# Moving the splits, gate rests and gate steps at the expert stages' seams, and the dilated values into the queries' and keys' block

## The chip, the cores and the metric

The kernel runs on one core of one Trainium2 chip. The metric is the device time of one launch in microseconds (us); lower is better.

## The reference

Two transformer layers on x of 512 tokens by 1024, in float32. The second layer begins with attention of two kinds over one projection, and both layers end with the same kind of expert stage (PEER), which the change touches most. Cut to what matters:

```python
def peer_ffn(h, w_query, sub_keys, expert_u, expert_v):
    def chunk(xc):                                   # 128 tokens
        q = (xc @ w_query).reshape(128, 8, 2, 128)
        s1 = einsum('thc,hnc->thn', q[:, :, 0], sub_keys[:, 0])
        s2 = einsum('thc,hnc->thn', q[:, :, 1], sub_keys[:, 1])
        v1, i1 = lax.top_k(s1, 16)
        v2, i2 = lax.top_k(s2, 16)
        cand = (v1[..., :, None] + v2[..., None, :]).reshape(128, 8, 256)
        top, ci = lax.top_k(cand, 16)
        eidx = e1 * 128 + e2                         # e1, e2: the chosen i1, i2
        gate = jax.nn.softmax(top, axis=-1)
        act = gelu(einsum('td,thkd->thk', xc, expert_u[eidx]))
        return einsum('thk,thkd->td', gate * act, expert_v[eidx])

# second layer, first half
h = rms_norm(x, norm1_g) * (1 + sc1) + sh1
qa, ka, va, qb, kb, vb, gl = jnp.split(h @ w_in, IN_SPLITS, axis=-1)
qa, ka = rope(rms_norm(qa)), rope(rms_norm(ka))      # dilated window attention, values va
qb, kb = rope(rms_norm(qb)), rope(rms_norm(kb))      # differential attention, values vb
```

There are 16384 experts, of which each of 8 heads picks 16 per token.

## The kernel before, in words

The program is one sequence of blocks; in a block, each engine has its own queue, in program order, and waits on semaphores; between two blocks all engines meet at a barrier (L83). Matmuls of float32 values are made of three with rounded halves: a tile is split into a high half (a cast on ScalarE) and a low half (a subtraction on VectorE), and hi*hi, lo*hi and hi*lo are added up.

**The expert stage** (`peer`, names p1 and p2 for the two layers) handles the first token tile (128 tokens) by fetching its experts' rows, and the other 384 tokens (DENSE) densely: all 128 tiles of 128 experts are multiplied with all 384 tokens, and a gate array that is zero for experts not chosen picks among them. Its blocks:

- `peer_queries` (p1q, p2q): the queries, then a `TurnedBack` guest.
- `peer_choose` (p1c, p2c): for each of four token tiles, TensorE makes 16 score products, and VectorE finds the top 16 by MAX8, FIND_INDEX8 and MATCH_REPLACE8. Between these steps stand the low-half splits of expert tiles, `A.split_lo` (L1429), at 14 places per token tile (EARLY); TensorE multiplies 14 tiles per token tile (`A.multiply`, L1439, output pre, double buffered), ScalarE takes them by a gelu (L1421), casts the high half of the tile four further on (L1410), and issues the store of the result (L1398). At the end of the choosing of a token tile, TensorE turns the choice (`turn`), and ScalarE copies it to the rows first, second and gate (L1557).
- `peer_gates` (p1g, p2g): the other 72 tiles, in 12 pieces (PIECES) of 6 tiles (LATE) and 8 steps (STEPS). A step makes one-hot rows of four tokens on VectorE (L1760, L1762), their rests on ScalarE (L1797), 8 products on TensorE (L1787) and a copy of the result by ScalarE (L1815). `steps_after(i)` says which steps follow tile i of a piece. Before the first step, `rest_of_gates` computes for all 384 tokens what rounding took from the gates (L1739 to L1745). VectorE also takes fetched expert rows (`fetch.take`, L1334, L1342), which GpSimd gathers (L1319). SyncE loads tile n + 4 when tile n has been split (L1389), and stores finished pieces.
- `peer_values` (p1v, p2v): for each of the 128 tiles, VectorE makes the weights w (L1908, L1910), w and the value tile are split (L1894, L1896, L1913, L1916), and TensorE adds up (L1931), after a rehearsal of ten small matmuls (L127).

In `peer_gates` the split order is one tile ahead at most: the first instruction of VectorE in the block is the split of the block's first tile.

**The second layer's start** (`block2`): `queries_keys` (qk) multiplies in 9 chunks of 512 columns (seven of queries and keys, two of the differential values vb), each of 8 slabs; the queries and keys are normed, rotated on VectorE (scratch prod, rot; tables rope) and turned. Four PSUM banks take the output, ScalarE copies each to raw (L3021). Then a `product` block of its own (va) makes the dilated values in two chunks, of 256 and of 512 columns (the latter with strided token tiles), eight banks, copies by ScalarE and VectorE (L361, L362), its SyncE also loading the masks. Then comes the dilated attention (dat).

What sets the order around the change is program order in these functions, by hand.

Of the kernel before, what the change touches and what calls it, by code (L numbers as in the profile page):

```python
# [1246 lines left out]
def peer(nc, tag, C, hT, ring, handed, wq, keysT, u_tab, u_rows, v_tab, gates, acts, take):  # L1247
# [3 lines left out]
    with ExitStack() as whole:  # L1251
# [4 lines left out]
        A = Activations(nc, whole, tag + "a", x_hi, x_lo, u_tab, acts)  # L1256
        with ExitStack() as mid:
# [5 lines left out]
            peer_choose(nc, tag + "c", C, qT, keys, rows, A, fetch)  # L1263
        kept = sbo("kept", [P, KEPT_PIECES, KEYS, PIECE])
        W = Weights(nc, whole, tag + "w", gates, acts, v_tab, A)
        peer_gates(nc, tag + "g", C, rows, gates, kept, A, W, fetch)
# [3 lines left out]
class Fetched:  # L1270
# [31 lines left out]
    def steps(self, tile):  # L1302

        late = KEYS - TT * EARLY
# [140 lines left out]
class Weights:  # L1445
# [4 lines left out]
    LOADS, G = 4, EGROUP  # L1450
    STORED = DENSE // PIECE - KEPT_PIECES

    def __init__(self, nc, ctx, tag, gates, acts, v_tab, A):
        sb, _, sem = phase_tools(nc, ctx, tag)
        self.gates, self.acts, self.v_tab, self.A = gates, acts, v_tab, A
        self.v = A.u
# [5 lines left out]
        self.w_made, self.v_ready = sem("w_made"), sem("v_ready")  # L1462
# [17 lines left out]


EARLY = 14


def peer_choose(nc, tag, C, qT, keys, rows, A, fetch):
# [4 lines left out]
    with ExitStack() as ctx:  # L1490
# [13 lines left out]
        chosen = sb("chosen", [P, 2, PAIRS])  # L1504
# [4 lines left out]
        gate = sb("gate", [P, PHEADS, TOPK])  # L1509
# [10 lines left out]
        @block.sync  # L1520
        def _(sp):
            for n in range(A.LOADS, TT * EARLY + A.LOADS):
                A.load(sp, n)

        def turn(pe, t):
            pe.wait_ge(chosen_ready, t + 1)
            if t >= 2:
                pe.wait_ge(moved, 3 * (t - 1))
            for n, src in enumerate((chosen[:, 0, :], chosen[:, 1, :], gate[:].rearrange("p h k -> p (h k)"))):
                last = nc.tensor.transpose(tp[:, n, 0:P], src, C["ident"][:])  # L1530
            last.then_inc(turned, 1)

        @block.tensor
        def _(pe):
# [15 lines left out]
            turn(pe, TT - 1)  # L1550

        @block.scalar
        def _(act):
# [15 lines left out]
            take_rows(TT - 1)  # L1569

        @block.vector
        def _(dve):
            n = 0
            for t in range(TT):
                dve.wait_ge(scored, t + 1)
# [3 lines left out]
                A.split_lo(dve, t * EARLY)  # L1579
                dve.wait_ge(step, n)  # L1580
                for j in range(HALVES):
                    if j == HALVES // 2:
                        A.split_lo(dve, t * EARLY + 1)
# [6 lines left out]
                A.split_lo(dve, t * EARLY + 2)  # L1590
# [4 lines left out]
                A.split_lo(dve, t * EARLY + 3)  # L1595
# [3 lines left out]
                A.split_lo(dve, t * EARLY + 4)  # L1599
# [13 lines left out]
                A.split_lo(dve, t * EARLY + 5)  # L1613
                dve.wait_ge(step, n)
                for h in range(PHEADS):
                    if h == PHEADS // 2:
                        A.split_lo(dve, t * EARLY + 6)
# [4 lines left out]
                A.split_lo(dve, t * EARLY + 7)  # L1622
# [10 lines left out]
                A.split_lo(dve, t * EARLY + 8)  # L1633
# [34 lines left out]
                for s in range(2):  # L1668
# [4 lines left out]
                    A.split_lo(dve, t * EARLY + 9 + 2 * s)  # L1673
# [5 lines left out]
                    A.split_lo(dve, t * EARLY + 10 + 2 * s)  # L1679
# [6 lines left out]
                A.split_lo(dve, t * EARLY + 13)  # L1686
# [15 lines left out]
def peer_gates(nc, tag, C, rows, gates, kept, A, W, fetch):  # L1702
# [10 lines left out]
    LATE = (KEYS - TT * EARLY) // PIECES  # L1713
    STORED = PIECES - KEPT_PIECES
    base = TT * EARLY
    with ExitStack() as ctx:
# [3 lines left out]
        gate_hi = hot1[:, 0].rearrange("p q k -> p (q k)")[:, 0:DENSE]  # L1720
        spare = W.g[:, 1].rearrange("p a g t -> p (a g t)")
        gate_rest, floor, gate_top = (spare[:, n * DENSE:(n + 1) * DENSE] for n in range(3))
        prod = ps("prod", [P, RING, TOK, KEYS])
        A.place(ps)
        hot_ready, hot_free, prod_free = sem("hot_ready"), sem("hot_free"), sem("prod_free")
        step, top_made, rest_known, rest_ready = (sem(n) for n in ("step", "top_made", "rest_known", "rest_ready"))
        stored = [sem(f"stored{s}") for s in range(KEPT_PIECES)]
        block = ctx.enter_context(nc.Block())

        def steps_after(i):  # L1730

            return range(STEPS * i // LATE, STEPS * (i + 1) // LATE)

        def rest_of_gates(dve):

            V = nc.vector
            ch = Chain(dve, step)
            dve.wait_ge(top_made, 1)
            ch.add(V.tensor_copy(gate_top, gate_hi))  # L1739
            ch.add(V.tensor_scalar(floor, gate_hi, TINY, None, ALU.max))  # L1740
            ch.add(V.tensor_tensor(gate_rest, gate[:], gate_hi, ALU.subtract))
# [1612 lines left out]
```

## Time and profile before

| | |
|---|---|
| median of 3 runs | 3777.59 us (3773.73 to 3779.41) |
| the profiled execution, its own time | 3770.69 us |
| its span in the profile | 3768.9 us |
| TensorE busy | 3595.0 us, 95% |
| VectorE busy | 2971.7 us, 79% |
| ScalarE busy | 1723.8 us, 46% |
| GpSimd busy | 753.1 us, 20% |
| DMA | 853.50 MB, 226 GB/s on average |

The span is the time from the first to the last profiled instruction. Busy time of TensorE (PE) counts matmuls, whose ends are modelled: a row of 128x384 lasts longer than the distance to the next. The chain that ended last is in its final 14% the value matmuls of the second expert stage.

### The profile page before, as it was taken

To read this page: it belongs to the slowest core of one execution; us is meant where nothing else is said; L and a number is where in the kernel's file an instruction comes from. 1 tells how busy PE (TensorE), PEld (TensorE's weight loads), DVE (VectorE), ACT (ScalarE), POOL (GpSimd) and SP (SyncE) were. 2 spreads that over 40 slices of the span, in tenths; PEclk is the share of its full clock that TensorE was granted. 3 is DMA by queue.
4 is the path that set the end of the run, shared out by engine and by line. 5 is a ranking of instruction groups with operands and counts; after the bars stand their busy time and mean duration, and the time that the engine had idled before them with its cause. 6 is when DMAs were issued, how large, how long until landed. Compare 5 with 4: busy or idle time off the path is not lost. (4 is left out here: it accounts for less than half of the span.)

```text
span 3768.9 us, 54814 instructions
## 1 busy us (share of the span) xinstructions
PE 3595.0 (95%) x19530; PEld 3150.1 (84%) x19530; DVE 2971.7 (79%) x6556; ACT 1723.8 (46%) x3277; POOL 753.1 (20%) x523
## 2 busy tenths in 40 slices
PE   8868999999999999999899989899999999999999
PEld 7546788899999988888788757788999999888887
DVE  4674653998988799999676495546998888899998
ACT  4424443333666633333344564343335666433333
POOL 0000000000333344444100000000003333355542
PEclk9989999999999999999999999999999999999999
DMA  4352323445999899999522102323558999899997
GB/s 149 138 172 89 102 68 101 136 161 185 303 309 308 292 371 404 405 404 401 189 84 79 51 1 90 109 73 121 163 165 276 310 309 311 321 405 404 404 403 293
DMA packets 371888, 853.50 MB, mean 226 GB/s; under 512 B 35728, under 2 KB 184848, under 8 KB 368912
## 3 DMA queue, kind: packets, MB, share of 16 engines
q1 hardware_dynamic: 258912, 530.84, 40.2%
q0 software_dynamic: 73728, 268.47, 18.8%
q10 hardware_dynamic: 38976, 50.68, 4.0%
q8 instruction: 157, 2.57, 0.3%
q14 instruction: 115, 0.94, 0.1%
HBM read 753.26 MB, written 95.42 MB: 225 GB/s over the span
## 5 line engine op out<-in xcount | busy, mean ns | idle before, releaser
L1319 POOL DMA_INDIRECT p2f_row<-in_expert_u_rows,p2f_index x128 | 176.9, 1382 | 1299.5 <-POOLq L83 1027.9
L1319 POOL DMA_INDIRECT p1f_row<-in_peer_u_rows,p1f_index x128 | 172.9, 1351 | 966.8 <-POOLq L83 684.3
L1931 PE MATMUL p2v_out<-p2a_u_hi,p2v_w_hi 128*128 128x512 f32 x768 | 298.9, 389 | 0.4 <-DVE p2v_w_lo L1916 0.4
L1931 PE MATMUL p1v_out<-p1a_u_hi,p1v_w_hi 128*128 128x512 f32 x768 | 298.9, 389 | 0.4 <-DVE p1v_w_lo L1916 0.4
L1931 PE MATMUL p1v_out<-p1a_u_hi,p1v_w_lo 128*128 128x512 f32 x768 | 298.8, 389 | 0.0
L1931 PE MATMUL p2v_out<-p2a_u_hi,p2v_w_lo 128*128 128x512 f32 x768 | 298.8, 389 | 0.0
L1931 PE MATMUL p1v_out<-p1a_u_lo,p1v_w_hi 128*128 128x512 f32 x768 | 298.8, 389 | 0.0
L1931 PE MATMUL p2v_out<-p2a_u_lo,p2v_w_hi 128*128 128x512 f32 x768 | 298.8, 389 | 0.0
L1319 POOL DMA_INDIRECT p2f_row<-in_expert_v,p2f_index x128 | 201.1, 1571 | 238.0 <-DVE p2f_sum L1342 216.4
L1319 POOL DMA_INDIRECT p1f_row<-in_peer_v,p1f_index x128 | 197.0, 1539 | 237.5 <-DVE p1f_sum L1342 217.0
L1894 ACT CAST p2a_u_hi<-p2a_u 128x1024 fp32r<-128x1024 f32 x128 | 135.0, 1055 | 186.8 <-PE p2v_out L1931 169.4
L1894 ACT CAST p1a_u_hi<-p1a_u 128x1024 fp32r<-128x1024 f32 x128 | 135.0, 1055 | 177.9 <-PE p1v_out L1931 168.7
L1439 PE MATMUL p1g_pre<-p_x_hi,p1a_u_hi 128*128 128x384 f32 x576 | 198.0, 344 | 3.8 <-DVE p1a_u_lo L1429 3.8
L1439 PE MATMUL p2g_pre<-p_x_hi,p2a_u_hi 128*128 128x384 f32 x576 | 197.2, 342 | 3.8 <-DVE p2a_u_lo L1429 3.8
L1439 PE MATMUL p1g_pre<-p_x_hi,p1a_u_lo 128*128 128x384 f32 x576 | 194.2, 337 | 0.0
L1439 PE MATMUL p1g_pre<-p_x_lo,p1a_u_hi 128*128 128x384 f32 x576 | 194.1, 337 | 0.0
L1439 PE MATMUL p2g_pre<-p_x_hi,p2a_u_lo 128*128 128x384 f32 x576 | 193.7, 336 | 0.0
L1439 PE MATMUL p2g_pre<-p_x_lo,p2a_u_hi 128*128 128x384 f32 x576 | 193.2, 336 | 0.0
L1342 DVE SCALAR_TENSOR_TENSOR p2f_sum<-p2f_row,p2f_weight,p2f_sum 128x1024 f32<-128x1024 f32 x127 | 162.5, 1280 | 11.7 <-DMA p2f_row<-in_expert_v,p2f_index 10.5
L1342 DVE SCALAR_TENSOR_TENSOR p1f_sum<-p1f_row,p1f_weight,p1f_sum 128x1024 f32<-128x1024 f32 x127 | 162.6, 1280 | 11.5 <-DMA p1f_row<-in_peer_v,p1f_index 9.7
L1931 PEld LDWEIGHTS p1v_out<-p1a_u_hi,p1v_w_hi 128*128 128x128 f32 x768 | 144.2, 188 | 30.5 <-DVE p1a_u_lo L1913 0.6
L1931 PEld LDWEIGHTS p2v_out<-p2a_u_hi,p2v_w_hi 128*128 128x128 f32 x768 | 144.2, 188 | 30.4 <-DVE p2a_u_lo L1913 0.6
(760 smaller groups left out, 10785.5 us busy)
## 6 DMA issues: line engine op xcount, KB each, us to landing
p1a_u<-in_peer_u SPq DMA_DIRECT2D x128, 512.0 KB
p1a_u<-in_peer_v SPq DMA_DIRECT2D x128, 512.0 KB
p2a_u<-in_expert_u SPq DMA_DIRECT2D x128, 512.0 KB
p2a_u<-in_expert_v SPq DMA_DIRECT2D x128, 512.0 KB
gates<-p_kept SPq DMA_DIRECT2D x20, 2048.0 KB
acts<-p1a_a ACTq DMA_DIRECT2D x128, 192.0 KB
p1w_a<-acts SPq DMA_DIRECT2D x128, 192.0 KB
acts<-p2a_a ACTq DMA_DIRECT2D x128, 192.0 KB
```

Of the source, the lines that this page charges most:

```text
L1319: self.nc.gpsimd.indirect_dma_start(self.row[:, n % self.RING, :], None, self.u_rows if dot else self.v_rows, bass.IndirectOffsetOnAxis(ap ...
L1342: V.scalar_tensor_tensor(self.sum[:], row, weight, self.sum[:], ALU.mult, ALU.add).then_inc(self.used, 1)
L1439: last = self.nc.tensor.matmul(self.pre[:, n % 2, 0:DENSE], u[:, s, k * P:(k + 1) * P], x[:, k, P:SEQ], start=(m == 0), stop=(m == 3 * DK ...
L1894: nc.scalar.copy(v_hi[:, n % VSLABS, :], v[:, n % LOADS, :]).then_inc(v_hi_ready, 1)
L1931: last = nc.tensor.matmul(out[:, o, :], lhs[:, s, t * P:(t + 1) * P], rhs[:, n % VSLABS, cols], start=(n == 0 and m == 0), stop=(n == KEYS ...
```

## The change

Parts, in order of the program:

1. `choice`: the chosen numbers and the gates of a token tile (chosen, gate), before scratch of `peer_choose`, now lie in `fetch.sum`, so that they outlive the block.
2. `peer_choose`: VectorE splits tiles 0 and 1 ahead of the loop, and each later place splits the tile two further on (`first_split`). One tile more is multiplied in the block (tile 56; INTO = 57). The last turn and its row copies leave it.
3. `peer_gates`: 71 tiles. VectorE splits tile INTO + 1 + i at iteration i. TensorE turns the last choice behind its first tile; ScalarE copies the rows at i = 1; VectorE waits for them at i = 2. The gates are rounded and their rests made per 128 tokens, at i = 0, 16 and 40. The 96 steps follow tiles 1 to 70 evenly, none the first. Values 0 and 1 are split here, on ScalarE behind tile TILES - 2 and ahead of the last gelu, on VectorE at the end.
4. `peer_values`: the splits of values 0 and 1 are gone from its loop.
5. `queries_keys`: 11 chunks; the last two are the dilated values, copied to va by ScalarE. prod and rot lie in va, the rope tables in the masks' buffer, and the masks are loaded when all rotations are done. The va block is gone.

```diff
+EARLY, AHEAD = 14, 2
+INTO = TT * EARLY + 1
...
@@ peer_choose
-            turn(pe, TT - 1)
+            A.multiply(pe, TT * EARLY)
...
-            take_rows(TT - 1)
+            A.gelu(act, TT * EARLY)
...
+            for ahead in range(AHEAD):
+                A.split_lo(dve, ahead)
             for t in range(TT):
+                first_split = t * EARLY + AHEAD
                 dve.wait_ge(scored, t + 1)
                 for j in range(HALVES):
                     V.max(val[:, j // 2, j % 2, 0:8], score[:, j, :]).then_inc(step, 1)
                 n += HALVES
-                A.split_lo(dve, t * EARLY)
+                A.split_lo(dve, first_split)
...
@@ peer_gates
+            return range(ALL * max(i - 1, 0) // (TILES - 1), ALL * i // (TILES - 1))
...
         def _(dve):
-            for t in range(PIECES):
-                for i in range(LATE):
-                    A.split_lo(dve, base + t * LATE + i)
-                    if t == 0 and i == 0:
-                        rest_of_gates(dve)
...
+            for i in range(TILES):
+                if i == 2:
+                    dve.wait_ge(rows_taken, 3)
+                if i in REST_AT:
+                    rest_of_gates(dve, ch, REST_AT.index(i))
+                if INTO + AHEAD - 1 + i < KEYS:
+                    A.split_lo(dve, INTO + AHEAD - 1 + i)
...
+            for n in range(W.AHEAD):
+                W.split_lo(dve, n)
...
         def _(pe):
+            for i in range(TILES):
+                A.multiply(pe, INTO + i)
+                if i == 0:
+                    turn_choice(nc, C, *choice, tp).then_inc(turned, 1)
...
         def _(act):
+            round_gates(act, 0)
+            for i in range(TILES):
+                for s in steps_after(i):
+                    rest_of_hot(act, s)
+                if i == TILES - 1:
+                    act.wait_ge(A.pre_ready, KEYS - A.SLABS + W.AHEAD)
+                    W.split_hi(act, W.AHEAD - 1)
+                A.gelu(act, INTO + i)
+                if i == 1:
+                    act.wait_ge(turned, 1)
+                    for n in range(3):
+                        nc.scalar.copy(rows[n][:, DENSE - P:DENSE], tp[:, n, 0:P]).then_inc(rows_taken, 1)
...
@@ peer_values
-                act.wait_ge(v_in[n % LOADS], 16 * (n // LOADS + 1))
-                nc.scalar.copy(v_hi[:, n % VSLABS, :], v[:, n % LOADS, :]).then_inc(v_hi_ready, 1)
+                if n >= W.AHEAD:
+                    W.split_hi(act, n)
...
@@ queries_keys
-    ALL = NC_ + 2
+    chunks = [(w_qk[c], False, None) for c in range(NC_)]
+    chunks += [(w_v[n], False, None) for n in range(2)] + w_va
+    ALL = len(chunks)
...
+            sp.wait_ge(rotated, TT * NC_)
+            for n, (to, source) in enumerate(transfers):
+                sp.dma_start(to, source).then_inc(transferred, 16)
+                sp.wait_ge(transferred, 16 * (n + 1))
...
-                nc.scalar.copy(raw[:, c % 2, t, :], out[:, t, :]).then_inc(raw_ready, 1)
+                to = raw[:, c % 2, t, :] if dst is None else dst(t)
+                nc.scalar.copy(to, out[:, t, 0:src.shape[2]]).then_inc(raw_ready, 1)
...
@@ block2
-            product(nc, "va", C, hT, DK, SEQ,
```

How the queues move, in the second layer (names p2). VectorE at the start of the choosing, before:

```order
L362 COPY p2m_qT<-p2q_out 128x512 x2
L172 UNCONDITIONAL_BRANCH
L1571 UNCONDITIONAL_BRANCH
L1577 MAX p2c_val<-p2c_score 128x8 x16
L1429 TENSOR_TENSOR p2a_u_lo<-p2a_u,p2a_u_hi 128x1024
```

and now:

```order
L362 COPY p2m_qT<-p2q_out 128x512 x2
L172 UNCONDITIONAL_BRANCH
L1587 UNCONDITIONAL_BRANCH
L1431 TENSOR_TENSOR p2a_u_lo<-p2a_u,p2a_u_hi 128x1024 x2
L1596 MAX p2c_val<-p2c_score 128x8 x16
L1431 TENSOR_TENSOR p2a_u_lo<-p2a_u,p2a_u_hi 128x1024
```

Two splits stand ahead of the 16 maxima, and the split behind them is that of tile 2.

VectorE from the end of the choosing into the gates, before (the branches are the barrier between the blocks; ISA is a fetched row's product):

```order
L1694 TENSOR_TENSOR p2c_gate<-p2c_weight,p2c_rtotal 128x128
L1490 UNCONDITIONAL_BRANCH
L1747 UNCONDITIONAL_BRANCH
L1429 TENSOR_TENSOR p2a_u_lo<-p2a_u,p2a_u_hi 128x1024
L1739 CAST p2w_g<-p2g_hot 128x384
L1740 TENSOR_SCALAR p2w_g<-p2g_hot 128x384
L1741 TENSOR_TENSOR p2w_g<-p_gateT,p2g_hot 128x384
L1743 RECIPROCAL p2w_g<-p2w_g 128x384
L1745 TENSOR_TENSOR p2w_g<-p2w_g 128x384
L1760 TENSOR_SCALAR p2g_hot<-iota,p_firstT,p2w_g 128x128 x4
L1762 TENSOR_TENSOR p2g_hot<-iota,p_secondT 128x512
L1334 ISA p2f_row,p2f_dots<-p2f_row,p2f_x 128x1024
```

and now:

```order
L1713 TENSOR_TENSOR p2f_sum<-p2c_weight,p2c_rtotal 128x128
L1509 UNCONDITIONAL_BRANCH
L1769 UNCONDITIONAL_BRANCH
L1762 TENSOR_SCALAR p2w_g<-p2w_g 128x128
L1763 TENSOR_TENSOR p2w_g<-p_gateT,p2w_g 128x128
L1765 RECIPROCAL p2w_g<-p2w_g 128x128
L1767 TENSOR_TENSOR p2w_g<-p2w_g 128x128
L1431 TENSOR_TENSOR p2a_u_lo<-p2a_u,p2a_u_hi 128x1024
L1336 ISA p2f_row,p2f_dots<-p2f_row,p2f_x 128x1024
L1336 ISA p2f_dots 128x1
L1431 TENSOR_TENSOR p2a_u_lo<-p2a_u,p2a_u_hi 128x1024
L1785 TENSOR_SCALAR p2g_hot<-iota,p_firstT,p2w_g 128x128 x4
```

The rests are a third as wide; the first fetched row and a second split now stand ahead of the first one-hots.

ScalarE over the same seam, before:

```order
L1410 CAST p2a_u_hi<-p2a_u 128x1024
L1398 DMA acts<-p2a_a 128x384
L1557 COPY p_firstT<-p2c_tp 128x128
L1557 COPY p_secondT<-p2c_tp 128x128
L1557 COPY p_gateT<-p2c_tp 128x128
L1490 UNCONDITIONAL_BRANCH
L1800 UNCONDITIONAL_BRANCH
L1802 CAST p2g_hot<-p_gateT 128x384
L1797 ACTIVATE p_x_hi<-p2g_hot,p2w_g 128x128 x4
L1421 ACTIVATE p2a_a<-p2g_pre 128x384
```

and now:

```order
L1822 CAST p2w_g<-p_gateT 128x128
L1423 ACTIVATE p2a_a<-p2g_pre 128x384
L1412 CAST p2a_u_hi<-p2a_u 128x1024
L1400 DMA acts<-p2a_a 128x384
L1832 ACTIVATE p_x_hi<-p2g_hot,p2w_g 128x128 x4
L1423 ACTIVATE p2a_a<-p2g_pre 128x384
L1412 CAST p2a_u_hi<-p2a_u 128x1024
L1400 DMA acts<-p2a_a 128x384
L1848 COPY p_firstT<-p2g_tp 128x128
L1848 COPY p_secondT<-p2g_tp 128x128
L1848 COPY p_gateT<-p2g_tp 128x128
L1860 COPY p_kept<-p2g_prod 128x128x4
```

The three row copies, last in the block of choosing before, now stand behind the gelu, the cast and the store of the gates' second tile, and ahead of the first step's copy.

## Rows read from the trace of the kernel before

**Rows 1.** The page, part 1: busy us of each engine (share of the span) and instructions.
```profile
PE 3595.0 (95%) x19530; PEld 3150.1 (84%) x19530; DVE 2971.7 (79%) x6556; ACT 1723.8 (46%) x3277; POOL 753.1 (20%) x523
```
**Rows 2.** Waits of TensorE, 2580 to 3245: us in total, times, longest.
```profile
PE p2c_pre L1439 <- DVE p2a_u_lo L1429: 6.1, 3, 4.5
PE p2g_pre L1439 <- DVE p2a_u_lo L1429: 3.8, 1, 3.8
PE p2c_score L1539 <- PEq L83: 1.7, 1, 1.7
...
PE p2g_prod L1787 <- ACT p_x_hi L1797: 1.3, 1, 1.3
PE p2g_prod L1787 <- ACT p_x_lo L1797: 0.4, 1, 0.4
PE p2v_out L1931 <- DVE p2v_w_lo L1916: 0.4, 1, 0.4
```
**Rows 3.** Waits of TensorE, 660 to 1325, the first expert stage.
```profile
PE p1g_prod L1787 <- ACT p_x_hi L1797: 1.2, 1, 1.2
PE p1g_prod L1787 <- ACT p_x_lo L1797: 0.9, 1, 0.9
```
**Rows 4.** Windows: length, busy of PE, PEld, DVE, ACT, POOL; granted clock, DMA, GB/s.
```profile
2844.00:2849.00 5.00, 4.87 (x19) 4.88 (x20) 4.93 (x10) 0.00 (x0) 3.69 (x4) 0.66 0.77 264
...
946.00:951.00 5.00, 5.00 (x23) 5.00 (x24) 5.00 (x11) 3.20 (x8) 2.08 (x2) 0.66 0.90 322
```
**Rows 5.** Timeline of TensorE, 2839.6 to 2844.5: start, duration, then idle before.
```profile
2839.66 0.34 PE L1439 MATMUL p2c_pre<-p_x_hi,p2a_u_lo 128*128 128x384 f32 x1
...
2844.13 0.44 PE L1439 MATMUL p2g_pre<-p_x_hi,p2a_u_hi 128*128 128x384 f32 x1 [3.80 <-DVE p2a_u_lo L1429]
```
**Rows 6.** Timeline of ScalarE, 2836 to 2843, into the gates.
```profile
2836.26 1.04 ACT L1410 CAST p2a_u_hi<-p2a_u 128x1024 fp32r<-128x1024 f32 x1
...
2840.42 1.04 ACT L1410 CAST p2a_u_hi<-p2a_u 128x1024 fp32r<-128x1024 f32 x1
...
2842.82 0.51 ACT L1802 CAST p2g_hot<-p_gateT 128x384 fp32r<-128x384 f32 x1 [0.87 <-PEq L83]
```
**Rows 7.** Timeline of VectorE, single rows from the second choosing and gates.
```profile
2586.85 3.26 DVE L1577 MAX8 p2c_val<-p2c_score 128x8 f32<-128x128 f32 x16 [4.79 <-PE p2c_score L1539]
...
2600.92 1.22 DVE L1429 TENSOR_TENSOR p2a_u_lo<-p2a_u,p2a_u_hi 128x1024 fp32r<-128x1024 f32 x1
...
2623.70 0.27 DVE L1629 TENSOR_TENSOR p2c_shifted<-p2c_top 128x128 f32<-128x128 f32 x1
...
2662.86 1.22 DVE L1429 TENSOR_TENSOR p2a_u_lo<-p2a_u,p2a_u_hi 128x1024 fp32r<-128x1024 f32 x1
...
2845.11 2.55 DVE L1743 RECIPROCAL p2w_g<-p2w_g 128x384 f32<-128x384 f32 x1
```
**Rows 8.** Timeline of ScalarE in the second choosing.
```profile
2582.97 3.88 ACT L1410 CAST p2a_u_hi<-p2a_u 128x1024 fp32r<-128x1024 f32 x4 [1.70 <-PEq L83]
2586.88 1.28 ACT L1421 ACT_TABLE_LOAD   x1
...
2630.99 0.31 ACT L1568 ACTIVATE p2c_weight<-p2c_shifted 128x128 f32<-128x128 f32 x1
```
**Rows 9.** Timeline of TensorE from keys to dilated values.
```profile
2077.33 0.39 PE L2996 MATMUL qk_out<-qk_w_lo,qk_x_hi 128*128 128x512 f32 x1
...
2082.15 0.71 PE L252 MATMUL va_out<-va_w_hi,va_x_hi 128*128 128x256 f32 x4 [0.36 <-ACT va_w_hi L310]
```
**Rows 10.** Timeline: GpSimd's first gather, and VectorE's first use of a row.
```profile
2843.47 1.41 POOL L1319 DMA_INDIRECT p2f_row<-in_expert_u_rows,p2f_index  x1 [1027.92 <-POOLq L83]
...
2849.82 1.21 DVE L1334 CUSTOM_DVE_ANT_0 p2f_row<-p2f_row,p2f_x 128x1024 f32<-128x1024 f32 x1
```
**Rows 11.** Windows of VectorE alone: length, busy, granted clock, DMA, GB/s.
```profile
2843.00:3235.00 392.00, 339.78 (x695) 1.00 0.91 304
```
**Rows 12.** Waits of SyncE over the span.
```profile
SPq L172 <- DMA b2v_masks<-in_masks: 6.4, 1, 6.4
```

More of the change, by code:

```diff
@@ L1521, in _ @@
         def _(sp):
-            for n in range(A.LOADS, TT * EARLY + A.LOADS):
+            for n in range(A.LOADS, INTO + A.LOADS):
                 A.load(sp, n)
@@ L1699, in _, with peer_gates @@
                     n += 1
-def peer_gates(nc, tag, C, rows, gates, kept, A, W, fetch):
+def peer_gates(nc, tag, C, rows, choice, gates, kept, A, W, fetch):
     first, second, gate = rows
@@ L1742, in rest_of_gates, with done_after @@
+        def done_after(steps):
+            return next(i for i in range(TILES) if ALL * i // (TILES - 1) >= steps)
+        def rest_of_gates(dve, ch, n):
+            V, cols = nc.vector, slice(n * P, (n + 1) * P)
+            dve.wait_ge(top_made, n + 1)
+            ch.add(V.tensor_scalar(floor[:, cols], gate_top[:, cols], TINY, None, ALU.max))
+            ch.add(V.tensor_tensor(gate_rest[:, cols], gate[:, cols], gate_top[:, cols], ALU.subtract))
             ch.wait()
-            ch.add(V.reciprocal(floor, floor))
+            ch.add(V.reciprocal(floor[:, cols], floor[:, cols]))
@@ new lines, in _ @@
+            ch = Chain(dve, step)
+            for i in range(TILES):
[6 more added lines that the diff above has]
+                for s in steps_after(i):
+                    r = s % RING
+                    if s >= RING:
+                        dve.wait_ge(hot_free, s - RING + 1)
+                    for q in range(TOK):
+                        token = s * TOK + q
+                        nc.vector.tensor_scalar(hot1[:, r, q, :], C["iota"][:, 0:KEYS], first[:, token:token + 1],
+                                                gate_top[:, token:token + 1], ALU.is_equal, ALU.mult)
+                    nc.vector.tensor_tensor(
+                        hot2[:, r], C["iota"][:, 0:KEYS].unsqueeze(1).broadcast_to([P, TOK, KEYS]),
+                        second[:, s * TOK:(s + 1) * TOK].unsqueeze(2).broadcast_to([P, TOK, KEYS]),
+                        ALU.is_equal).then_inc(hot_ready, 1)
+                for n in fetch.steps(i):
+                    fetch.take(dve, n)
@@ L2985, in _ @@
             rehearse(nc, C["ident"], out[:, 0, :])
-            for c in range(ALL):
+            for c, (src, stepped, _) in enumerate(chunks):
+                cols = src.shape[2]
                 for k in range(DK):
@@ L2995, in _ @@
                         for n, (xs, ws) in enumerate(((x_hi, w_hi), (x_lo, w_hi), (x_hi, w_lo))):
-                            last = nc.tensor.matmul(out[:, t, :], xs[:, k, t * P:(t + 1) * P], ws[:, s % SLABS, :],
+                            last = nc.tensor.matmul(out[:, t, 0:cols], xs[:, k, tile], ws[:, s % SLABS, 0:cols],
                                                     start=(k == 0 and n == 0), stop=(k == DK - 1 and n == 2),
@@ L3136, in block2 @@
+        values.close()
         obT = sb("obT", [P, DIFF_HEADS, SEQ])
```

249 lines of the change are left out of this document (123 added, 126 removed).

## The prediction, made before the changed kernel was run

> **What bounds the kernel now.** I read the page first: TensorE is busy 95% of the span [rows 1], so only stretches in which it stands still or runs at half clock can give time back. Next, TensorE's waits in the second expert block [rows 2] and, of the first, those that differ [rows 3]; its waits for VectorE's split, 6.1 and 3.8, are the same there. Then the granted clock right behind the long waits [rows 4] and the timelines of the seams [rows 5 to 9]. The reader is to see that nothing inside the long stages waits: all losses sit within some 30 us of a seam, where TensorE waits for VectorE's low half of an expert tile (u_lo) or for the one-hot rows of a gate step. TensorE takes 4.16 us for a tile (two casts behind consecutive tiles start 4.16 apart [rows 6]).
>
> **Queries to choosing.** Before, VectorE takes the 16 first maxima from 2586.85 and only then splits tile 0, so TensorE, whose scores end at 2586.8, idles 4.5 of the 6.1 us [rows 2, 7]. Now two splits stand ahead of the maxima. ScalarE casts four tiles in 3.88 from 2582.97 [rows 8], so the first two are cast by 2584.9 and split by some 2586.3, while VectorE stands idle for the scores anyway (4.79 [rows 7]). Cover: that idle time. The idle of 4.5 goes, twice: **9.0**. The granted clock over the 5 us behind it is 0.66, as in four more stretches of which two are shown [rows 4], TensorE at its 1.2 GHz level for most of it, which costs 0.34 x 5 = 1.7; it goes with the idle: **3.4**. The other 1.6 of the 6.1 are two later tiles waiting for VectorE: **3.2**. A restart also costs some 0.27 that the waits don't show: the first matmul lasts 0.44, and an idle is counted from a modelled end 0.16 late [rows 5]; three restarts go per block: **1.6**.
>
> What is late next there? TensorE starts 4.5 us earlier, VectorE does not, but it is two tiles ahead. Tile 4 is ready where tile 2's split stands now, 2600.92 + 1.22 = 2602.1 [rows 7]; TensorE wants it at 2586.85 + 4 x 4.16 = 2603.5. Tile 18 is ready at 2662.86 + 1.22 = 2664.1; wanted at 2586.85 + 18 x 4.16 + 3.8 for the scores = 2665.5. Margins of 1.4, tight, positive. The exponential: its input is ready at 2623.97 [rows 7]; ScalarE, now waiting for it, then needs 0.31, a table load of 1.28 and a gelu of 0.5, done at 2626.1; TensorE needs that for tile 9 at 2628.1. The table load ahead of the exponential isn't in this sum, since a load runs before its instruction's wait is over: at 2586.88 one ran before TensorE had begun the tile of its gelu [rows 8]. I take no wait here.
> The Trainium skill (ScalarE: Activation LUTs, What ACT_TABLE_LOAD costs) says that a switch costs 1283 ns and some 1380 ns of drain, about 2.66 us. The trace shows the first part and not the second: the exponential at 2630.99 stands right behind its load [rows 8]. By the page, with both switches behind the wait, ScalarE would be done at 2630.1, tile 9 2.0 late in each block, and my sum 4.0 smaller.
>
> **Choosing to gates.** Tile 56 moves into the choosing, the last turn and its three row copies into the gates. Before: TensorE ends at 2840.3, ScalarE at 2841.95, the barrier lets go at 2842.8 (0.87 [rows 6]), the split takes 1.2, TensorE starts at 2844.13: 3.8 idle [rows 5]. Now tile 57 is already split; what is left is the last tile's gelu and cast (to 2840.42 + 1.04 = 2841.46, the tile's modelled end being 2840.0) and the barrier, 0.87: 2.3. Gain 1.5 x 2 = **3.0**. Whether the clock still falls is unknown: behind the 1.7 before the scores [rows 2] the matmuls kept their speed, behind 3.8 it was 0.66 [rows 4]. 2.3 lies between; of the ends 0 and 1.7 a block I take the middle, 0.85; gain **1.7**.
> Then the steps. Let s be the barrier's release. VectorE: gate rests of 128 columns instead of 384 (the reciprocal alone was 2.55 [rows 7]; about a third, 1.8 in all), split of 58 to s+3.0, then the first fetched row. GpSimd issues it 0.65 behind the release and takes 1.41; it was used without a wait at s+7.0 [rows 10]. I put its landing at s+5, an estimate between the ends s+2.1 and s+7.0; two either way move the wait below by as much, down to none. Row, split 59 and step 0's one-hots end at s+9.0, ScalarE's rests at s+10.2; TensorE, through tile 58 at s+9.0, waits 1.2. At tile i=2 VectorE waits for ScalarE's three row copies, which stand behind gelu, cast and store of tile 58, to s+12.2: behind that wait are split 60 and step 1's one-hots, and TensorE waits 0.9 for them. So 2.1 a block, 4.2 in all, against 1.2 + 0.9 plus a half-clock stretch of 1.7 from 946 [rows 3, 4] and 1.3 + 0.4 [rows 2]: 5.5. Gain **1.3**. The rests at i=16 and 40 (1.8 on VectorE) cost nothing: VectorE is busy 339.8 of 392 us there [rows 11]; without that cover 3.6 a block. The new spread of the 96 steps: the same matmuls, zero.
>
> **Gates to values.** Values 0 and 1 are now split inside the gates; ScalarE's second cast stands ahead of the last gelu, so the block may end a little later (I take 0.2, a fifth of a cast, as most of it fits into ScalarE's wait for that tile). The first value matmul waited 0.4 for w_lo [rows 2]; now the rehearsal ends last. Gain **0.4** for both blocks.
>
> **Dilated values.** The same 192 matmuls move into the loop of queries and keys. What goes is the block's start: from the last matmul at 2077.33 (0.23 to the next) to 2082.15 = **4.6** [rows 9]. ScalarE now makes all copies, with four banks instead of eight; I take nothing for it, since a bank is written again only after three others and the loop's changes of chunk show no wait now. The 1.5 MB of masks are issued with the last weights, some 20 us before the end; they made SyncE wait 6.4 before [rows 12], so they are hidden; if not, up to 6.4 is lost.
>
> **Sum:** 9.0 + 3.4 + 3.2 + 1.6 + 3.0 + 1.7 + 1.3 + 0.4 + 4.6 = 28.2. The profiled execution took 3770.69 (span 3768.9), 6.9 under the median of the three runs, 3777.59; from that one to 3742.5, from the median to **3749**. A measurement tells 0.2% (7.6 us) from no change.
>
> **Rivals.**
> - *Gates open no better.* Row landing and the rows_taken wait take what the seam gives: without 3.0, 1.7 and 1.3, 22.2 gained, 3755. For it: the fetches compete with tile loads just there. Against: tile 57 needs nothing. 0.13.
> - *VectorE becomes the bound in the choosing.* A margin of 1.4 fails and TensorE's earlier start is waited out: without 9.0 and 3.2, 16.0 gained, 3762. For: VectorE is busy nearly throughout. Against: no long TensorE wait behind tile 4 before, and two tiles' lead. 0.10.
> - *The values don't join*: bank or mask waits give back 4.6: 3754. 0.05.
> - *Both table switches behind the wait* (the load does not run ahead, and each lasts about twice its 1.28): 4.0 less, 24.2 gained, 3753. This is the Trainium skill's rule above. 0.04.
> - *Does not do what it says*: first, second and third rival together, 28.2 - 6.0 - 12.2 - 4.6 = 5.4 gained, 3772. 0.05.
> - *Slower.* In the gates a split two tiles on needs a cast made behind a tile only three back, before four. If VectorE stands at it each tile, cast and VectorE's work come in series: 339.8/72 + 1.04 = 5.76 against TensorE's 392/72 = 5.44, 0.32 over 142 tiles = 45 lost: 3777.6 - 28.2 + 45 = 3794. It decides from 0.20 per tile (28.2/142), and 0.25 makes it slower by 0.2%. Against: casts are made some 2 us behind their tile. 0.03.
>
> **Numbers.** The forecast has 0.60, over 3743 (no fall of the clock, 1.7, and no waits in the gates, 4.2) to 3753. The range 3740 to 3762 starts 3 us below that, half the spread of the three runs, and takes in the first four rivals: 0.92. It could stop at 3755 with 0.82 in it, but VectorE's margin of 1.4 is the least certain bound, so I let it reach there. Faster by over 0.2%: 0.60 + 0.13 + 0.10 + 0.05 + 0.04 = 0.92; within: 0.05; slower: 0.03.
>
> **What would show it.** TensorE's first choosing tile right behind the scores, with granted clock 1.0; no wait for u_lo in the choosing; 2.3 idle before tile 57; two waits of about 1 us before gate steps 0 and 1, with VectorE waiting before split 60; no block between keys and dilated attention. Wrong: u_lo waits near tiles 4 or 18, waits for u_lo or one-hots in mid-gates, or a wait before the dilated scores over 2 us.

## The result, and the profile after

The kernel before took 3775.74 us (median of 4 runs, 3773.73 to 3779.41), the changed one 3863.06 us (4 runs, 3858.42 to 3866.96). The ratio is 1.0235, 95% interval 1.0222 to 1.0247: 2.3% slower, where 3749 us was forecast. The profiled run took 3866.96 us (span 3865.2).

The page of the changed kernel, part 1, and of part 2 the granted clock and the traffic in 40 slices (PE is TensorE, PEld its weight loads, DVE VectorE, ACT ScalarE, POOL GpSimd, SP SyncE; a q behind a name is the engine's queue, which issues and waits):

```profile
PE 3638.5 (94%) x19510; PEld 3186.2 (82%) x19510; DVE 2967.5 (77%) x6558; ACT 1715.6 (44%) x3277; POOL 665.4 (17%) x523
...
PEclk9889999999999999999999999999999989999999
...
GB/s 146 159 143 97 89 74 102 165 165 206 272 277 263 276 344 402 401 400 399 192 85 85 39 33 67 109 98 132 165 189 265 274 240 267 314 403 402 400 398 297
```

The page nearly hides the loss. TensorE's share fell by a point only against [rows 1], because matmuls at half clock count as busy. The traffic tells the place: in the gates stages (slices 11 to 14 and 31 to 34) it is 240 to 277 GB/s, where those slices had 276 to 311 before.

A table of stages tells more. Each is counted from its first matmul to that of the next, so it holds the seam at its end; the last two columns are experiments told of below.

| stage, us | before | change | store 3 after | and 2 rows later |
|---|---|---|---|---|
| ahead of the first scores | 665.0 | 667.0 | 666.7 | 667.9 |
| first choosing (56, now 57 tiles) | 261.1 | 255.9 | 255.9 | 255.9 |
| first gates (72, now 71 tiles) | 394.5 | 443.3 | 390.2 | 388.2 |
| first values | 533.2 | 535.4 | 534.7 | 534.0 |
| queries, keys, dilated values | 253.8 | 248.7 | 248.8 | 248.9 |
| second choosing | 261.1 | 255.9 | 255.9 | 255.9 |
| second gates | 392.0 | 449.7 | 389.7 | 387.3 |
| second values | 532.8 | 533.8 | 534.9 | 532.1 |

In the first row nothing was edited; these traces differ there by up to 2.9 us, which tells what a small difference in one row is worth.

One tile (24 matmuls at 0.1735, 4.2 us) went from each gates stage to the choosing. With it the choosing gained 9.4 us in each block, and the values that joined 5.1. But the gates stages lost 53 and 62 us, tile for tile. Here are TensorE's waits in the second one (tiles p2g) from the changed kernel's waits over the span (us in total, times, longest), which answer to [rows 2]:

```profile
PE p2g_prod L1815 <- issue: 34.6, 10, 5.2
...
PE p2g_pre L1441 <- PEq L83: 2.5, 1, 2.5
...
PE p2g_prod L1815 <- ACT p_x_hi L1832: 2.3, 1, 2.3
```

Ten waits of 3.5 us on average, one for each piece that is stored, and "issue" names no releaser. Around all but the two shortest (0.7 and 0.8 us) the clock falls. Windows of the changed kernel around the first of them (columns as in [rows 4]):

```profile
2936.70:2941.70 5.00, 0.38 (x3) 0.09 (x2) 1.73 (x4) 2.80 (x7) 0.49 (x1) 0.74 1.02 416
2941.70:2946.70 5.00, 5.00 (x21) 5.00 (x22) 4.14 (x12) 4.18 (x11) 0.00 (x0) 0.50 0.77 305
```

So the 62 us are 35 of standing still and up to 27 of half clock: over the stage, the length times what the granted clock lacks of 1 gives 29, against 2 before. Who is late? The step waits for ScalarE's rests of the one-hot rows. ScalarE's timeline, 2930 to 2945 of the changed kernel:

```profile
2932.05 0.49 ACT L1423 ACTIVATE p2a_a<-p2g_pre 128x384 f32<-128x384 f32 x1 [1.98 <-PE p2g_pre L1441]
2938.90 1.04 ACT L1412 CAST p2a_u_hi<-p2a_u 128x1024 fp32r<-128x1024 f32 x1 [6.36 <-DMA p2a_u<-in_expert_u]
2938.92 0.33 ACTq L1400 DMA_DIRECT2D acts<-p2a_a  x1
2939.85 0.58 ACT L1860 COPY p_kept<-p2g_prod 128x512 f32<-128x512 f32 x1
2940.33 2.45 ACT L1832 ACTIVATE p_x_lo<-p2g_hot,p2w_g 128x128 fp32r<-128x128 f32 x8
```

ScalarE stands 6.4 us at a cast whose tile has not landed, and behind that cast in its order stand the store, the copy and the rests. TensorE runs on with the tiles already split until it needs the rests; it stands for 4.6 us, to 2941.70. So a transfer is late, and the transfers are in SyncE's order. SyncE's waits in the second gates stage, of the kernel before and then of the changed one (L1824 and L1873 are the same line, the store of a kept piece, which waits for ScalarE's last copy into it; in the changed kernel the view names the releaser of eight of its ten waits):

```profile
SPq L1389 <- DVE p2a_u_lo L1429: 228.9, 58, 7.8
SPq L1824 <- ACT p_kept L1815: 65.1, 10, 7.6
```

```profile
SPq L1391 <- DVE p2a_u_lo L1431: 183.4, 38, 8.1
SPq L1873 <- ACT p_kept L1860: 131.3, 8, 18.8
```

And around the next stall, from SyncE's and ScalarE's timelines of the changed kernel: the issue of the store, that of the load behind it, then ScalarE's cast of that tile:

```profile
2964.65 0.38 SPq L1873 DMA_DIRECT2D gates<-p_kept  x1
2965.07 7.30 SPq L1391 DMA_DIRECT2D p2a_u<-in_expert_u  x1
...
2980.46 1.04 ACT L1412 CAST p2a_u_hi<-p2a_u 128x1024 fp32r<-128x1024 f32 x1 [7.33 <-DMA p2a_u<-in_expert_u]
```

SyncE waits 16.4 us at a store instead of 6.5, on average. The load behind the store comes out slowly (7.30 us for an issue that takes 0.33 elsewhere; behind the stores of the kernel before it takes 5.9 to 7.9 too) and its tile is there 15.4 us after it. The load ahead of the store had been issued at 2947.71, so 32.8 us lie between a load and the landing of the next. By an estimate the loads' lead, four buffers of some 5.4 us each (392.0 us over 72 tiles), covers 22.

**Theory A**: the order in SyncE's queue. Before, low halves were split in the loop round of their own tile, and a store stood two rounds after the last step of its piece. Now the splits, which release the loads, run one round ahead, and the store stands one round after that step: SyncE comes to it two tiles sooner against the copy that it waits for (2 x 5.4 = 10.8 by the length of a tile; measured 16.4 - 6.5 = 9.9), and the loads queue up behind it. **Theory B**: the 2 MB stores crowd the loads on the DMA engines. **Theory C**: the new spread, in which a piece's 8 steps no longer begin with a tile.

### The profile page after: what moved, and what is told of

It reads as the page before. It is cut to its first block and busy times, and to the rows that moved or that the text cites. A ratio compares the mean times of both kernels' runs of the same rounds, so it can differ in the third digit from the quotient of the medians.

```text
span 3865.2 us, 54750 instructions
## 1 busy us (share of the span) xinstructions
PE 3638.5 (94%) x19510; PEld 3186.2 (82%) x19510; DVE 2967.5 (77%) x6558; ACT 1715.6 (44%) x3277; POOL 665.4 (17%) x523
## 5 line engine op out<-in xcount | busy, mean ns | idle before, releaser
L1321 POOL DMA_INDIRECT p2f_row<-in_expert_u_rows,p2f_index x128 | 163.3, 1276 | 1349.9 <-POOLq L83 1018.9
L1431 DVE TENSOR_TENSOR p2a_u_lo<-p2a_u,p2a_u_hi 128x1024 fp32r<-128x1024 f32 x128 | 156.2, 1221 | 87.1 <-ACT p2a_u_hi L1412 84.4
L1431 DVE TENSOR_TENSOR p1a_u_lo<-p1a_u,p1a_u_hi 128x1024 fp32r<-128x1024 f32 x128 | 156.2, 1221 | 80.7 <-ACT p1a_u_hi L1412 79.5
L1321 POOL DMA_INDIRECT p1f_row<-in_peer_v,p1f_index x128 | 165.2, 1290 | 280.1 <-DVE p1f_sum L1344 254.2
L1321 POOL DMA_INDIRECT p2f_row<-in_expert_v,p2f_index x128 | 164.0, 1281 | 286.8 <-DVE p2f_sum L1344 260.3
L1489 DVE TENSOR_TENSOR p1a_u_lo<-p1a_u,p1a_u_hi 128x1024 fp32r<-128x1024 f32 x128 | 156.4, 1222 | 33.6 <-ACT p1a_u_hi L1485 26.4
L1489 DVE TENSOR_TENSOR p2a_u_lo<-p2a_u,p2a_u_hi 128x1024 fp32r<-128x1024 f32 x128 | 156.3, 1221 | 30.7 <-ACT p2a_u_hi L1485 26.1
```

The lines of the kernel that those rows point to most:

```text
L1321: self.nc.gpsimd.indirect_dma_start(self.row[:, n % self.RING, :], None, self.u_rows if dot else self.v_rows, bass.IndirectOffsetOnAxis(ap ...
L1431: self.nc.vector.tensor_tensor(self.u_lo[:, s, :], self.u[:, n % self.LOADS, :], self.u_hi[:, s, :], ALU.subtract).then_inc(self.u_ready, 1)
L1489: self.nc.vector.tensor_tensor(self.v_lo[:, n % self.slabs, :], self.v[:, n % self.LOADS, :], self.v_hi[:, n % self.slabs, :], ALU.subtrac ...
```

## The experiments

**Theory A by the position alone.** The changed kernel, one constant changed in SyncE's order:

```diff
-                    if i == done_after((t + 1) * STEPS) + 1:
+                    if i == done_after((t + 1) * STEPS) + 3:
                         keep(t)
```

> The change, with each store of a kept piece put into SP's queue two tiles later (behind the load of the third tile after the piece's last step, instead of the first). Theory A (SP's order: the store waits for the last copy of its piece, and the loads of table tiles stand behind it; the splits now run two tiles ahead, so SP comes to the store two tiles sooner than before and waits 16.4 us a time instead of 6.5): the ten stalls of 3 to 6 us in each gates stage go, each stage falls from 443 and 450 us to about 388, and the kernel to about 3746 us (3740 to 3755). Theory B (the 2 MB stores crowd the loads on the DMA engines) and theory C (the 96 steps now stand twice in a tile where the engines can't follow): no change in the stalls, 3850 to 3870 us.

Measured: 3755.44 us (3752.28 to 3757.26), ratio to before 0.9947 (0.993 to 0.9964). The bytes, the steps and their spread are as in the change; 108 us went. The stalls are gone. SyncE's waits, 2830 to 3219, and then TensorE's:

```profile
SPq L1391 <- DVE p2a_u_lo L1431: 255.6, 58, 8.6
SPq L1873 <- ACT p_kept L1860: 35.3, 9, 4.8
```

```profile
PE p2g_pre L1441 <- PEq L83: 2.5, 1, 2.5
PE p2g_prod L1815 <- ACT p_x_hi L1832: 1.7, 2, 1.0
```

In this trace the load behind the store is again slow (issued at 2904.52, landed at 2920.58, the store itself at 2919.02), but the load ahead of it was issued at 2898.79: 21.8 us between, about the cover, and no cast waits for a load. B and C fall as causes of the loss, since bytes and spread stayed; that the 2 MB ahead of a load are part of its lateness is shown by the halved store below.

**One tile between the two.** The same constant at + 2.

> The change, with each store of a kept piece one tile later in SP's queue (two tiles after the piece's last step; the change has one, the fast run three). Theory A: SP waits one tile (5.5 us) less than in the change, 11 us a time, and with 7 us of issue behind the store the loads are late by what is left of a tile: some short stalls stay, 3760 to 3800 us. If only the bytes or the steps mattered it would be at 3755 or at 3860.

Measured: 3757.23 us (3754.95 to 3759.73). Less stayed than expected: SyncE waits 69.3 us in 8 waits (8.7 each), the casts 8.3 us for loads, and TensorE has one stall of 1.4 us. The loss is not proportional to the wait; it begins where wait and landing pass the four tiles' cover.

**The other way round.** The kernel before, its store two tiles sooner:

```diff
-                    if 1 <= t <= STORED and i == 1:
-                        keep(t - 1)
+                    if t < STORED and i == LATE - 1:
+                        keep(t)
```

> The kernel before, with each store of a kept piece two tiles sooner in SP's queue (in the piece's last tile instead of the second tile of the next). Theory A: SP waits 16 us a time there instead of 6.5, the casts wait for the loads, and the kernel before becomes slower by 50 to 115 us (3825 to 3890). Theory C (the new spread of the steps is needed for the loss): within 10 us of 3776.

Measured: 3991.25 us (3986.24 to 3993.41), ratio 1.0572 (1.0554 to 1.059). Nothing of the change is in this kernel, and it loses 217 us where the change lost 87. TensorE's stalls in the second gates stage are 78.7 us in 10. SyncE's and then ScalarE's waits, 2959 to 3455:

```profile
SPq L1389 <- DVE p2a_u_lo L1429: 203.6, 39, 8.2
SPq L1824 <- ACT p_kept L1815: 189.2, 10, 20.7
```

```profile
ACT p2a_a L1421 <- PE p2g_pre L1439: 120.7, 60, 3.6
ACT p2a_u_hi L1410 <- DMA p2a_u<-in_expert_u: 97.1, 12, 11.1
```

18.9 us a wait and up to 11.1 at a cast: the wait was larger than my 16, and the loss out of my range; why the same two tiles cost this kernel so much more isn't shown. Theory C, by which the new spread is needed, falls here once more.

**The store out of SyncE's queue.** ScalarE issues it behind its own last copy of a piece; SyncE only loads.

```diff
+                    if q == STEPS - 1 and t < STORED:
+                        keep(act, t)
...
-                for t in range(STORED):
-                    if i == done_after((t + 1) * STEPS) + 1:
-                        keep(t)
```

> The change, with the stores of the kept pieces issued by ScalarE right behind its last copy of the piece, so that SP's queue holds nothing but loads. Theory A: as with the store three tiles after or a little better, 3740 to 3750 us, and the 131 us of SP's waits at the store are gone. Theories B and C: 3850 to 3870 us, since the bytes, their time and the steps stay.

Measured: 3857.93 us (3850.89 to 3863.01), as slow as the change; my expectation missed by over 100, and by the time alone the run would speak for theory B or C. The trace tells otherwise. SyncE's wait at the store was gone, as meant, and no cast waits for a load any more (48.2 us in 9 in the change). The loss came back elsewhere: ScalarE's timeline, 2968.5 to 2977.5 of this kernel:

```profile
2968.55 0.38 ACTq L1837 DMA_DIRECT2D gates<-p_kept  x1
...
2971.86 1.04 ACT L1412 CAST p2a_u_hi<-p2a_u 128x1024 fp32r<-128x1024 f32 x1
2972.00 4.86 ACTq L1400 DMA_DIRECT2D acts<-p2a_a  x1
2976.95 0.59 ACT L1866 COPY p_kept<-p2g_prod 128x512 f32<-128x512 f32 x1 [4.05 <-issue]
```

The next store of activations, behind 2 MB in the same engine's queue, takes 4.86 us to issue instead of 0.33, and ScalarE computes nothing meanwhile (47.0 us in 9 waits, up to 7.5). TensorE's stalls are 31.5 us in 10. SyncE can bear such an issue, since it computes nothing; ScalarE can't.

**The wait back at SyncE, without the store.** As the last, and SyncE waits at its old place for the piece's last copy and issues nothing there.

> The stores of the kept pieces are issued by ScalarE as in the run before, but SP still waits at its old place for the last copy of the piece, with nothing to issue there. Theory A: the wait alone makes the loss, so as slow as the change, 3850 to 3870 us. Theory B: the store isn't where it was and nothing crowds the loads otherwise, so as fast as the run before.

Measured: 3955.19 us (3950.98 to 3969.3), 97 us more than the run before it, for a wait of SyncE and nothing else. The time is out of my range. The 97 us are near the change's loss, but the trace doesn't show A's way: SyncE waits there for 92.4 us in 10 waits, and still no cast waits for a load. What grew is ScalarE's own loss, its waits behind a store in the second gates stage:

```profile
ACT p_kept L1866 <- issue: 81.4, 9, 12.7
```

They were 47.0 in the run before. SyncE, released by the same copy as ScalarE's store, issues three loads within 0.9 us (from 3029.36), and the store of activations behind the 2 MB then takes ScalarE 11.6 us to issue, at 3032.81. So the wait costs, but this pair neither tests nor shows that late loads are how; that rests on the position alone and on the halved store.

**The store in two halves** at the change's place, the second half behind the next load:

```diff
-                    if i == done_after((t + 1) * STEPS) + 1:
-                        keep(t)
+                    for half in range(2):
+                        if i == done_after((t + 1) * STEPS) + 1 + half:
+                            keep(t, half)
```

> The change with each store of a kept piece in two halves of 1 MB, the first at the old place (behind the wait of 16.4 us), the second behind the load of the next tile. Theory A in its full form (the load behind the store is late by the wait of 16.4 us and by the 6 to 7 us that its own issue takes behind 2 MB in the queue, together more than the four tiles of cover): with 3 us of issue in place of 7 the stalls of PE shrink from 3.4 to under 1.5 us, 3770 to 3830 us. If the wait alone counts, 3863 as the change.

Measured: 3793.68 us (3787.81 to 3795.79). SyncE waits nearly as long as in the change (14.3 us on average), but TensorE's stalls in the second block are 10.9 us in 6 instead of 34.6 in 10. So the lateness of a load has two parts, the wait for the copy and the 2 MB ahead of it in its queue; cutting the first removed the stalls, cutting the second most of them. SyncE's waits, 2849 to 3260:

```profile
SPq L1875 <- ACT p_kept L1860: 142.9, 10, 17.2
```

**The dilated values alone**, that part of the diff on the kernel before.

> The kernel before with the dilated values inside the queries' and keys' block and nothing else of the change. The forecast had 4.6 us for it, the stage in the profile of the change shows 5.0: 3769 us (3767 to 3771), and no other stage moves. If the gain were given back in the stages behind, 3774.

Measured: 3770.9 us (10 runs, 3765.6 to 3776.31), ratio 0.9993 (0.9984 to 1.0003). The stage went from 253.8 to 250.5 us in this profile, and 248.7 to 250.5 in those of the kernels that have the change. The medians' difference, 2.9 us, can't be told from nothing by this interval, so the gain stands on the stage's length and not on the whole time.

**The seam to the values.** With the stalls gone the kernel was at 3755 and not at 3749. Of the rest the trace shows one place: TensorE idles 3.46 us ahead of the values, 1.43 before, and the first matmuls behind it, the rehearsal, run at half clock. Windows of the kernel with the store three tiles after:

```profile
3215.97:3219.60 3.63, 0.17 (x3) 0.06 (x2) 0.37 (x1) 0.96 (x2) 0.00 (x0) 0.87 0.51 191
3219.60:3224.60 5.00, 5.00 (x22) 4.90 (x23) 3.78 (x9) 1.96 (x3) 0.95 (x1) 0.50 0.52 160
```

I first took it for a transfer in flight at the stage's end (theory D), and made two kernels, both on top of the store three after. One issues the last store of activations in the next stage:

```diff
         self.split_hi(act, n + self.SLABS)
-        self.store(act, n)
+        if n not in (INTO - 1, KEYS - 1):
+            self.store(act, n)
```

> The kernel with the store three tiles after, and the last store of activations of the choosing and of the gates stage issued at the beginning of the next stage instead of at the end of its own. Theory D (a stage ends only when the last transfer it issued has landed: 3218.76 us for a PE that starts at 3219.59): the idle at the seam to the gates falls from 2.5 to about 1 us and at the seam to the values from 3.5 to 1.5, with less half clock behind them: 3742 to 3750 us. Rival (the last copy or the last cast ends the stage): 3755 as without it.

Measured: 3755.36 us (3753.69 to 3756.66); the idles are 2.50 and 2.96 us. The other moves the load:

```diff
-            sp.wait_ge(rest_ready, PIECES * STEPS)
-            W.load_gates(sp, 1)
...
             A.stores_landed(sp, KEYS)
+            W.load_gates(sp, 1)
```

> The kernel with the store three tiles after, and the load of the second group of gates (640 KB, issued 1.3 us before the last store of activations) issued at the beginning of the values stage. Theory D: the last store shares the DMA engines with nothing, lands in about 2 us instead of 3.3, and the seam to the values loses 1 to 2 us of idle and some half clock in each block: 3748 to 3753 us. Rival: no change, 3755, or slower where the load is missed by the values stage (it is needed twelve tiles, some 50 us, later).

Measured: 3755.8 us (3754.08 to 3758.36), idle 3.32. Theory D fell. The trace also holds the engines' drains, their last records ahead of the barrier, which the views leave out. At the end of the gates stage they name the late one (kernel with the store three after; start, end, engine; TensorE's ends at 3216.18):

```
3215.12 3216.38 DVE DRAIN
3216.18 3216.97 ACT DRAIN
3208.36 3218.83 POOL DRAIN
```

GpSimd drains until 3218.83. Its last gather there was issued at 3209.43; before, at 3224.51, with a drain until 3233.67 and ScalarE's until 3235.30, so there it did not matter. GpSimd's timeline, 3200 to 3225:

```profile
3207.38 1.74 POOL L1321 DMA_INDIRECT p2f_row<-in_expert_u_rows,p2f_index  x1 [7.40 <-DVE p2f_dots L1336]
3209.43 0.94 POOL L1321 DMA_INDIRECT p2f_row<-in_expert_v,p2f_index  x1 [0.30 <-issue]
```

It waits for VectorE's last use of a fetched row, 12.4 us ahead of TensorE's last product before and 8.9 now. Theory E: move two gathers into the values stage.

```diff
-            for n in range(FETCHED_IN_GATES + fetch.RING):
+            for n in range(FETCHED_IN_GATES + fetch.RING - 2):
...
-            for f in range(FETCHED_IN_GATES + fetch.RING, 2 * PAIRS):
+            for f in range(FETCHED_IN_GATES + fetch.RING - 2, 2 * PAIRS):
```

> The kernel with the store three tiles after, and the last two gathers that GpSimd issues in the gates stage issued in the values stage instead. Theory E (GpSimd's drain ends 9.4 us after the issue of its last gather, at 3218.83, while ScalarE's ends at 3216.97, and the stage ends with the later; the change had moved that gather 2.5 us nearer to the end): the idle at the seam to the values falls from 3.5 to about 1.5 us as in the kernel before, and the transposes behind it run at full clock: 2 to 5 us less in each block, 3745 to 3752 us. Rival (the gather isn't what holds the seam, or it is missed in the values): 3755 or more.

Measured: 3750.59 us (3746.21 to 3752.62), ratio 0.9938 (0.9924 to 0.9951). The range just touches that of the kernel without the edit (3752.28 to 3757.26), so the gain of 4.9 stands on the traces: the gates and values stages are together 7.9 us shorter in the table. In the second block the idle is back at 1.58 and the clock full. TensorE's timeline, and windows, of this kernel:

```profile
3215.14 2.02 PE L127 MATMUL p2v_out<-ident 128*128 128x128 f32 x16 [1.58 <-PEq L83]
```

```profile
3213.28:3215.14 1.86, 0.28 (x3) 0.17 (x3) 0.48 (x1) 1.07 (x2) 0.00 (x0) 1.00 0.92 361
3215.14:3220.10 4.96, 4.96 (x32) 4.47 (x33) 3.73 (x9) 1.92 (x3) 3.73 (x3) 1.00 0.61 194
```

In the first block the idle fell as well, from 3.41 to 1.59, but there the clock still falls: 0.69 over 1311.97 to 1316.97. So the clock does not follow the length of the idle alone.

**The seam to the gates.** ScalarE's drain there ends with its last cast. On top of the store three after:

```diff
+        if n != INTO - 1:
             self.split_hi(act, n + self.SLABS)
...
             round_gates(act, 0)
+            A.split_hi(act, INTO - 1 + A.SLABS)
```

> The kernel with the store three tiles after, and the last cast of the choosing stage (1.04 us, behind the last gelu on ScalarE) issued at the beginning of the gates stage. Theory: ScalarE's drain ends with that cast (2828.91 us) and holds the seam of 2.5 us; it falls to 1.6, and as the clock stays full behind the idle of 1.7 us ahead of the scores, some half clock goes too: 1 to 3 us less in each block, 3750 to 3754 us. Rival: another engine ends the stage, and nothing changes (3755).

Measured: 3754.12 us (3751.48 to 3757.96), a gain of 1.3 that the runs can't tell from none; the idle fell from 2.50 to 2.11 and not to 1.6, and what ends the stage then isn't shown. Both seams together:

> Both edits of the two runs before on top of the store three tiles after: the sum of both, 3741 to 3751 us; the fastest of all kernels here.

Measured: 3749.41 us (3742.79 to 3752.63), ratio 0.9934 (0.9921 to 0.9948). It is the fastest median here, 0.7% under the kernel before and 2.9% under the change; from two rows later alone it can't be told.

## Why the prediction was wrong

**The step that failed** is the sum of the gates stages. It had a gain of 1.3 at their opening and for the rest of the loop the clause "The new spread of the 96 steps: the same matmuls, zero." The two stages lost 53 and 62 us, tile for tile. The spread itself did not cost that: with the store three tiles after it is the same, and the stages take 390.2 and 389.7 us. What the sum put at nothing, without a reason, was SyncE's store between the loads. I costed the moved splits and steps on VectorE, ScalarE and TensorE, and did not follow SyncE's queue, although the store's place against the steps had gone from two rounds to one and the load is released by the split, which had moved by another. The numbers for it stood in the trace of the kernel before: SyncE waited 65.1 us in 10 waits at L1824, and casts already waited 12.0 us in 9 for loads, so the cover was nearly used up. A moved store between loads needed its own term, 9.9 us a time, against a cover of four tiles.

**The rivals.** The slower one, 3794 us at 0.03, had VectorE and the cast in series. VectorE did wait for casts in the changed kernel's second gates stage (82.4 us in 39 waits), but as a consequence of late loads; with the store three after, 22.2 us in 28 waits stay and cost TensorE nothing. So that rival had the right sign by a mechanism that did not act, its time was 69 us too low, and the mechanism that decided had no rival.

**Terms that held, and two that did not.** *Queries to choosing*, 9.0, 3.4, 3.2 and 1.6: TensorE's waits in the second choosing, 2626 to 2881 of the changed kernel, are down to

```profile
PE p2c_score L1555 <- PEq L83: 1.7, 1, 1.7
PE p2c_pre L1441 <- ACT p2a_a L1423: 0.8, 1, 0.8
```

and behind the scores the clock is full:

```profile
2626.00:2631.00 5.00, 5.00 (x41) 5.00 (x42) 3.62 (x9) 4.98 (x5) 0.00 (x0) 1.00 0.35 111
2631.00:2640.00 9.00, 9.00 (x54) 9.00 (x53) 9.00 (x50) 2.92 (x5) 0.00 (x0) 1.00 0.49 160
```

VectorE did not become the bound. The idle to the gates was forecast at 2.3 and is 2.50. Together the choosing stages gave 18.9 us against 20.2 (the first four terms and the 3.0). The wait of 0.8, in each block, is one I did not have: I had a margin of 2.0 at the first token tile's exponential and did not look at the fourth's, which waits for VectorE. ScalarE's timeline there, 2846 to 2855 of the changed kernel:

```profile
2846.44 1.28 ACT L1584 ACT_TABLE_LOAD   x1
2851.79 0.31 ACT L1584 ACTIVATE p2c_weight<-p2c_shifted 128x128 f32<-128x128 f32 x1 [4.07 <-DVE p2c_shifted L1648]
2852.12 1.28 ACT L1423 ACT_TABLE_LOAD   x1
2853.41 0.49 ACT L1423 ACTIVATE p2a_a<-p2c_pre 128x384 f32<-128x384 f32 x1
```

The first table load runs ahead of its instruction's wait, as the forecast took it, and the second costs its 1.28 us and nothing more: the gelu begins 0.01 behind it. So the rival of both switches behind the wait fell. The Trainium skill (ScalarE: Activation LUTs, What ACT_TABLE_LOAD costs) has 1.38 us of drain beside each load, and this trace shows none.

*Clock behind the seam to the gates*, 1.7 for an even chance: it stays at 1.00 from 2881.70 to 2892.90 in the changed kernel, so both falls of before are gone and the term gave 3.4. *Gates' opening*, 1.3 gained, did not come: the waits ahead of the first step are 2.2 and 2.3 us where 2.1 was forecast, but behind each the clock falls (0.66 over 934 to 939, 0.67 over 2893 to 2898), 1.7 us a block that I did not have. So the opening costs 7.9 in both blocks, against 5.5 before. *Dilated values*, 4.6: the stage fell by 5.1 in the changed kernel and by 3.3 to 5.1 over all traces; the masks cost no wait.

**A term of the wrong sign.** *Gates to values*, 0.4 gained: in the changed kernel the idle there is 3.38 and 3.05 us where it was 1.43, and the clock behind it is 0.50 and 0.66 over 5 us, where it was 1.00. I had looked at ScalarE's second cast, and the late one was GpSimd, whose last gather follows VectorE's last use of a row. Its repair gave 4.9 us by the medians.

With the store and this seam repaired the changed kernel takes 3750.6 us, 23.6 us under the 3774.2 of the kernel before measured beside it, where 28.2 was forecast. That is no credit, since one of the two repairs mends a term that was forecast: the change as it stands is 87 us slower than the kernel before, and the forecast's range left no room for a queue that was not followed.

## What to carry to other kernels

When work is moved in a loop, write down for each queue what stands between two loads, what releases each, and how far the loads run ahead. Here a wait in a queue of loads cost next to nothing until wait and landing passed the buffers' cover, and then a stall, mostly with half clock behind it, for every round; one round in the position of a store decided 106 us. Look for regular stalls in TensorE's waits: their number (10, the stored pieces) points at the loop that makes them. And when a run comes out at the time that a theory names, look in its trace whether it got there by that theory's way: the store issued by ScalarE did not.

## What the runs showed of the hardware

- A transfer issued by the same engine right behind a 2 MB store takes 5.9 to 7.9 us to issue instead of 0.33 in the kernel before, and 6.2 to 8.0 in the changed one, both on SyncE. It lands behind the store: in the kernel with the store three after, 11.5 to 16.1 us after its issue, where the three loads of the same 0.5 MB ahead of the store at 2903.95 took 4.5 to 5.4. Behind 1 MB, in the halved store, the issue took 3.8 at the median. Which resource is full isn't shown.
- An engine that computes and issues stands still for such an issue (ScalarE, up to 7.7 us, and up to 13.7 with SyncE's loads released at the same moment).
- GpSimd's drain at a stage's end ended 9.2 to 10.3 us after its last gather was issued, in three traces; when the store and the load still in flight there were moved, the idle stayed at 3.0 and 3.3 us.
- The granted clock behind an idle of TensorE does not follow the idle's length alone. Over the 5 us behind 3.5 and 4.6 us it was 0.50 (the 1.2 GHz level); behind 2.5 us at the seam to the gates 1.00, but behind 2.2 and 2.3 us ahead of the first step 0.66 and 0.67; behind the same idle of 1.6 us at the seam to the values 0.69 in the first block and 1.00 in the second.
